# Split-weight products in a two-block layer kernel: three matmuls of 256 columns for each weight tile, in one half of a PSUM bank

## The reference

```
# first block
proj  = rms_norm(x) @ w_in;  mixed = g_nsa*(o_nsa @ w_up_nsa) + g_dn*(o_dn @ w_up_dn)
x     = x + mixed @ w_o
x     = x + (silu(h2 @ w_ffn_gate) * (h2 @ w_ffn_up)) @ w_ffn_down;   x = rms_norm(x)
# second block
proj  = rms_norm(x) @ w_in_2;  x = x + concat(y_rwkv, y_mla) @ w_out_2
x     = x + (silu(conv(h @ w_gate_2)) * (h @ w_up_2)) @ w_down_2;   return rms_norm(x)
```

## Time and profile before

| what | us |
|---|---|
| median of 3 runs | 2822.27 (2820.22 to 2822.9) |
| the profiled execution, its own time | 2820.33 |
| its span, first to last instruction | 2818.5 |
| TensorE busy with matmuls | 2771.2 (98%), 16660 matmuls |
| VectorE busy | 2023.7 (72%) |
| ScalarE busy | 1364.0 (48%) |
| GpSimd busy | 479.3 (17%) |

### The profile page before, as it was taken

One profiled execution on the slowest core, in us unless ns is written; L12 is line 12 of the kernel. 1 busy time (PEld: TensorE's weight loads), 2 busy tenths in 40 slices (PEclk: granted clock), 3 DMA queues, 4 the chain that ended last, 5 costly groups with the idle time before them and its releaser, 6 DMA issues.

```text
span 2818.5 us, 42260 instructions
## 1 busy us (share of the span) xinstructions
PE 2771.2 (98%) x16660; PEld 2434.1 (86%) x16660; DVE 2023.7 (72%) x3102; ACT 1364.0 (48%) x2051; POOL 479.3 (17%) x526
## 2 busy tenths in 40 slices
PE   8999999999999999999999999999999999999998
PEld 7888888888888888888888888878998888888887
DVE  7987797776776666656657888878677777667655
ACT  6453455455555445434435545434454444444434
POOL 2211011110111111001102635421111111001101
PEclk9999999999999999999999999999999999999999
DMA  6444333455555555555556534221365555555555
GB/s 227 162 160 159 121 116 132 145 191 188 193 187 190 192 191 191 192 190 193 188 183 199 177 124 133 92 76 53 120 202 191 191 192 189 193 188 194 189 180 164
DMA packets 133396, 474.65 MB, mean 168 GB/s; under 512 B 14800, under 2 KB 15056, under 8 KB 132944
## 3 DMA queue, kind: packets, MB, share of 16 engines
q1 hardware_dynamic: 133200, 471.96, 50.3%
HBM read 469.80 MB, written 2.10 MB: 167 GB/s over the span
## 4 chain that ended last, share of the span: by engine, by line
PE 90%; DVE 5%; ACT 2%; POOL 1%; issue 1%; DMA 0%; SPq 0%; DVEq 0%; ACTq 0%; POOLq 0%
PE ps L899 90%; DVE U L1869 1%; DVE ringl L1869 1%; POOL U L2551 1%; ACT high L1409 1%; PE ps L902 1%; POOL U L2624 0%; ACT U L1409 0%; DVE U L1878 0%; DVE xT L1869 0%; DMA xT<-in_x_dram 0%; DVE hx L1869 0%; DVE U L2067 0%; ACT hr L1409 0%; DVE U L1875 0%
## 5 line engine op out<-in xcount | busy, mean ns | idle before, releaser
L899 PE MATMUL ps<-hr,high 128*128 128x512 f32 x4672 | 1491.4, 397 | 11.8 <-DVE ringl L1869 10.8
L1869 DVE TENSOR_TENSOR ringl<-ring,high 128x1024 fp32r<-128x1024 f32 x888 | 1082.6, 1221 | 435.1 <-ACT high L1409 434.6
L1409 ACT ACTIVATE high<-ring 128x1024 fp32r<-128x1024 f32 x888 | 915.6, 1033 | 601.6 <-PE ps L899 590.7
L899 PEld LDWEIGHTS ps<-hr,ringl 128*128 128x128 f32 x4672 | 879.2, 188 | 192.5 <-issue 1.4
L899 PE MATMUL ps<-hr,ringl 128*128 128x256 f32 x4672 | 924.3, 279 | 0.0
L899 PEld LDWEIGHTS ps<-hr,high 128*128 128x128 f32 x4672 | 717.6, 188 | 21.0 <-issue 15.1
L899 PE MATMUL ps<-yur,high 128*128 128x512 f32 (+1 forms) x2432 | 682.9, 370 | 3.8 <-DVE xT L1869 2.2
L2551 POOL TENSOR_TENSOR U<-U,rs 128x256 f32<-128x256 f32 x292 | 264.5, 906 | 1688.3 <-DVE U L1869 1668.8
L899 PEld LDWEIGHTS ps<-yur,ringl 128*128 128x128 f32 x2176 | 400.0, 188 | 79.6
L1409 ACT ACTIVATE U<-ps 128x256 f32<-128x256 f32 (+3 forms) x481 | 172.8, 371 | 592.0 <-PE ps L899 567.6
L899 PE MATMUL ps<-yur,ringl 128*128 128x256 f32 x2176 | 429.9, 279 | 0.0
(11 more groups left out here) (178 smaller groups left out, 1250.2 us busy)
## 6 DMA issues: line engine op xcount, KB each, us to landing
ring<-in_w_dram SPq DMA_DIRECT2D x862, 512.0 KB, 3.3
ring<-in_w_dram SPq DMA_DIRECT2D x48, 256.0 KB, 3.3
xT<-in_x_dram SPq DMA_DIRECT2D x3, 512.0 KB, 8.1
out_dram<-hx SPq DMA_DIRECT2D x3, 512.0 KB, 2.7
cst<-in_cst_dram SPq DMA_DIRECT2D x1, 1374.5 KB, 12.5
yT<-in_lora_dram SPq DMA_DIRECT2D x1, 1024.0 KB, 7.4
xT<-in_x_dram SPq DMA_DIRECT2D x2, 256.0 KB, 4.5
U<-in_lora_dram SPq DMA_DIRECT2D x1, 512.0 KB, 5.4
```

What stands on the lines that cost most here:

```text
L899: return e.matmul(out, l, r, start=start, stop=stop)
L1409: return e.activation(out, i, ACT.Copy, scale=scale)
L1869: return e.tensor_tensor(out, a, b, op)
```

## The change

Every split product takes the narrow form. The high weights are used for two matmuls of 256 columns, over x's high half and over its low half; all three products of a tile are summed into half 0 of the bank. The order by pairs of tiles stays. Evacuation is then one step: ScalarE's copy signals `free` itself, VectorE's `rest` is gone, `wo` and `down` take one addition instead of two, and GpSimd's scaling waits for ScalarE instead of VectorE. For the units `up` VectorE waits for ScalarE's `free` before it multiplies with the gate. The planner's costs follow: TILE 0.348 to 0.342, ROWS 0.72 to 0.69 (the units with moving weights), and no additions of half 1 in VectorE's list. The number of weight tiles, the DMAs, the splits and the side chains stay as they are.

```diff
-TILE, TILE4, TILE33, ROWS = 0.348, 0.432, 0.23, 0.72
+TILE, TILE4, TILE33, ROWS = 0.342, 0.432, 0.23, 0.69
...
+            scaled_ = [u for u in ends if normed(u)]
+            added = [u for u in ends if sums_x(u)]
+            merged = [u for u in ends if u.kind == "up"]
...
-                                [("free" if one_half(u) else "half", u.i) for u in own] + [("data", u.i) for u in own if one_half(u)]))
-            work["DVE"].append((m - 0.5, sum(0.42 if u.kind == "wout" else 0.85 if sums_x(u) else 0.9 if u.kind == "up" else 0.43 for u in both_) + 0.4 * later.count("up"),
-                                [("end" if sums_x(u) else "half", u.i) for u in both_], [("free", u.i) for u in both_]))
-            work["POOL"].append((m - 0.5, 1.1 * len(both_), [("free", u.i) for u in both_], [("data", u.i) for u in both_]))
+                                [("free", u.i) for u in own] + [("data", u.i) for u in own if not normed(u)]))
+            work["DVE"].append((m - 0.5, 0.42 * len(added) + sum(0.9 if u.key[0] else 0.48 for u in merged) + 0.4 * later.count("up"),
+                                [("end", u.i) for u in added] + [("free", u.i) for u in merged], [("free", u.i) for u in added]))
+            work["POOL"].append((m - 0.5, 1.1 * len(scaled_), [("free", u.i) for u in scaled_], [("data", u.i) for u in scaled_]))
...
-                            c = mact if one_half(prev) else mdve
+                            c = mdve if sums_x(prev) else mact
                             e.wait_ge(c.sem, c.after("free", prev.i))
...
-                                if u.kind == "wout":
-                                    for n_, half in enumerate(moving(u, k0 + k)):
-                                        mm(out[:, 0:SEQ], wh, half, start and n_ == 0, False)
-                                else:
-                                    mm(shaped(out[:, :], 2, SEQ), wh, halves(u, k0 + k), start, False)
+                                for n_, half in enumerate(moving(u, k0 + k)):
+                                    mm(out[:, 0:SEQ], wh, half, start and n_ == 0, False)
...
-                copy(place_of(u), src).then_inc(mact.sem, mact.inc("free" if one_half(u) else "half", u.i))
+                copy(place_of(u), src).then_inc(mact.sem, mact.inc("free", u.i))
...
-            def rest(u, dst):
-
-                e.wait_ge(mact.sem, mact.after("half", u.i))
-                tt(dst, dst, ps[u.bank][:, SEQ:2 * SEQ], ADD).then_inc(mdve.sem, mdve.inc("free", u.i))
-
             def evac0(u):
                 key = u.key
-                if one_half(u):
-                    return
                 if u.kind == "up":
                     part, t = key
                     s = sg[t % 4]
-                    rest(u, um[:, t % 2, :])
                     e.wait_ge(mact.sem, mact.after("sig", 16 * part + t))
-                    e.wait_ge(mdve.sem, mdve.last())
+                    e.wait_ge(mact.sem, mact.after("free", u.i))
...
-                    parts = 1 if u.kind == "wout" else 2
-                    for j in range(parts):
-                        src = ps[u.bank][:, SEQ * j:SEQ * j + SEQ]
-                        if u.kind == "wo":
-                            i = stt(x, src, 0.5, x, MUL, ADD)
-                        else:
-                            i = tt(x, x, src, ADD)
-                        i.then_inc(mdve.sem, mdve.inc("free", u.i) if j == parts - 1 else mdve.inc())
-                        if j < parts - 1:
-                            e.wait_ge(mdve.sem, mdve.last())
+                    i = stt(x, src, 0.5, x, MUL, ADD) if u.kind == "wo" else tt(x, x, src, ADD)
+                    i.then_inc(mdve.sem, mdve.inc("free", u.i))
...
-                else:
-                    rest(u, place_of(u))
...
+                    e.wait_ge(mdve.sem, mdve.after("tb", f, t))
...
-                    e.wait_ge(mdve.sem, mdve.after("free", u.i))
+                    e.wait_ge(mact.sem, mact.after("free", u.i))
```

More of the change, by code:

```diff
@@ L766, in build, with normed @@
             needs[units[index[("rw", q, 0)]].first()] = [(f"rw{q % STREAMS}", (q // STREAMS - 2) * len(RECUR) + taken)]
-        def one_half(u):
-            return u.kind in ("cmpkc", "cmpvc", "vs", "vw", "uv", "uq", "uk")
         def sums_x(u):
             return u.kind in ("wo", "down", "wout")
+        def normed(u):
+            return u.kind in ("gates", "dn", "q", "kc", "vc", "ks", "kw", "mg", "gate", "fup", "lora", "rw", "lat")
         work = {"PE": [], "ACT": [], "DVE": [], "POOL": []}
@@ L800, in build @@
             own = [u for u in ends if not sums_x(u)]
-            both_ = [u for u in ends if not one_half(u)]
+            scaled_ = [u for u in ends if normed(u)]
+            added = [u for u in ends if sums_x(u)]
+            merged = [u for u in ends if u.kind == "up"]
             later = [u.kind for u in p.ends.get(m - 2, [])]
             work["ACT"].append((m - 0.5, 0.4 * len(own) + 0.4 * (later.count("mg") + later.count("up")), [("end", u.i) for u in own] + [("data", u.i) for u in p.ends.get(m - 2, []) if u.kind == "mg"],
-                                [("free" if one_half(u) else "half", u.i) for u in own] + [("data", u.i) for u in own if one_half(u)]))
-            work["DVE"].append((m - 0.5, sum(0.42 if u.kind == "wout" else 0.85 if sums_x(u) else 0.9 if u.kind == "up" else 0.43 for u in both_) + 0.4 * later.count("up"),
-                                [("end" if sums_x(u) else "half", u.i) for u in both_], [("free", u.i) for u in both_]))
-            work["POOL"].append((m - 0.5, 1.1 * len(both_), [("free", u.i) for u in both_], [("data", u.i) for u in both_]))
+                                [("free", u.i) for u in own] + [("data", u.i) for u in own if not normed(u)]))
+            work["DVE"].append((m - 0.5, 0.42 * len(added) + sum(0.9 if u.key[0] else 0.48 for u in merged) + 0.4 * later.count("up"),
+                                [("end", u.i) for u in added] + [("free", u.i) for u in merged], [("free", u.i) for u in added]))
+            work["POOL"].append((m - 0.5, 1.1 * len(scaled_), [("free", u.i) for u in scaled_], [("data", u.i) for u in scaled_]))
             work["POOL"].append((m, 0.0, [("used", m - 1)] if 0 < m <= M else [], []))
@@ L877, in place_of @@
             return (flat if u.kind == "uq" else kn)[:, key[0], :]
-        def normed(u):
-            return u.kind in ("gates", "dn", "q", "kc", "vc", "ks", "kw", "mg", "gate", "fup", "lora", "rw", "lat")
         rs_read = {"norm2": index[("mg", 1, 15)], "attn_g": index[("fup", 1, 43)], "ffn_g": index[("rw", 7, 2)],
                    "final_g": index[("fup", 2, 43)]}
[L887 to L891, removed]
         block = ctx.enter_context(nc.Block())
@@ L1922, in evac0 @@
                         mdve.also("sg", 16 + t)
-                elif u.kind in ("wo", "down", "wout"):
-                    x = xT[:, key[-1], :]
+                elif sums_x(u):
+                    x, src = xT[:, key[-1], :], ps[u.bank][:, 0:SEQ]
                     e.wait_ge(used.sem, used.after(u.end()))
```

## The result

The kernel before took 2821.24 us (median of 4 executions, 2819.47 to 2822.90), the changed one 2868.48 us (median of 4, 2866.27 to 2870.67): 1.0168 times as long, 95% interval 1.0150 to 1.0185. The forecast was 2790, in the range 2778 to 2818; the change costs 47 us instead of giving 32.

A forecast was written before the change was run, and what follows sets the result against it. The prediction took TensorE's matmul stream as the bound. Gains of 25.7 us in pure stream, 4.5 among side work and 2 from evacuation made 32 us less, a forecast of 2790 us, range 2778 to 2818.

The forecast's parts named there:

- What bounds the kernel: Whole span: TensorE, busy 98% at full clock, sets the time by its number of matmuls times their starting pace.
- The counts: Main stream: 6592 tiles, 3296 pairs, change form; 6592 more matmuls, 23252 in all, none of 512 columns in that stream.
- The pace of a pair: Main stream: a pair of tiles changes by between -11 and +15 ns from 0.690 us; 10.5 ns less taken for pure stream.
- the 2446 pairs in pure stream: Stretches of main stream alone, mostly feed-forward: each pair 10.5 ns shorter, 25.7 us less in all.
- The 850 pairs among side work: Mixed stages: each pair gains half the pure-stream amount, 5.3 ns, 4.5 us less in all.
- (c): Rival: w_out_2's first part, 117.5 ns a matmul, shows the narrow form's pace; +48 us, 2870 us; chance 0.04.
- (b): Rival: each matmul has a fixed cost besides its columns, so the third one slows a tile; 2839 us; chance 0.06.
- Evacuation: Emptying PSUM: VectorE loses 182 us of additions, hidden in pure stream; 2 us less in all, between 0 and 8.
- The planner's order: Mixed stages: side steps move against the main stream, a few microseconds to either side; taken as 0.

## Why the prediction was wrong, by its own steps

**What bounds the kernel**: right. TensorE's stream set the time before and after, no wait took its place, and the time moved with the pace of the starts. One reading was too smooth: a 9 in the clock's line of the earlier trace rows is 90% or more, and between 434 and 442 us the clock of the kernel before was at 0.57.

**The counts**: right, 23252 matmuls, none of 512 columns, 3296 pairs.

**The pace of a pair, the step that failed.** The prediction bounded it at -11 and +15 ns from two places of w_out_2 and took -10.5, because the second part "has the same blocks, no side work, and low inputs at the same kind of places". Measured over the feed-forward parts: 6 x 117.8 - 690 = +16 to +17 ns, just past the other bound. With 3296 pairs that is 53 us if every pair ran so; the account gives 39, and w_o and parts of 620 to 730 us did run at 113.33. That is the term of 25.7 us less for the 2446 pairs in pure stream, with its sign wrong. What was wrong was not an omitted cost: the narrow form's 113.33 was real, and is read in the same place after the change. It was one of two paces of the same instructions, and one stretch of 60 us, a single unbroken run of the stream, was taken as 530 samples where it was one. In three of the later kernels that very stretch, at the same distance, ran at 117.78, so it was chance that the trace of before showed it fast. The two places of the earlier trace rows disagreed by 4%, in a trace whose wide form repeats its mean pace within 0.3 ns a matmul from one feed-forward part to the other (900 / 5210 against 700 / 4058 us); that disagreement was the finding, and I explained it away by side chains and shared blocks. `vs`, which I counted as a second witness, reads its operands the other way round, so it was no witness for this distance.

**The 850 pairs among side work**, -5.3 ns each: wrong in sign too. Among the side work most restarts came out slow.

**The rivals.** (c), given 0.04, named the size: +48 us, 2870, against 2868. That it is so close is in part luck: it has all 48 from the pace, which gave 39, and knows nothing of the middle stretch's part. Its wording, that the slow pace is the narrow form's own and the fast one the exception, holds for distance 16 in 91 of 101 stretches, but not as a property of the form: at 48 the first feed-forward part runs at 113.33. (b), a fixed cost for each matmul, 2839, is not what was seen: one form has paces from 113.3 to 120.0 at one count of matmuls, by place alone. The Trainium skill, "TensorE: Matmul & The Clock Gate", section "Back-to-back issue gap", gives N / 2.4 + 2.5 ns as the gap of an isolated matmul, which comes to 109.2 for 256 columns. The runs show 113.3 to 120.0, and nothing in that formula depends on where the operands lie.

**Evacuation**, 2 us less: not found. VectorE fell by 125 us and not by 182; the additions went as counted (`xT` from 224 to 128), but its other steps grew longer, the remainders written into `yur` from 419 to 675 ns on the mean, with idle time before them for ScalarE's rounding. None of it matters in a stream that doesn't wait for VectorE, as the prediction said. GpSimd's scalings are released by ScalarE, as foreseen.

**The planner's order**, taken as nothing: it cost. With the new evacuation the side chains' part grew and the clock fell to half for some 20 us from 1968 us on; against the run with the split alone it is 8 us, 6 in the profiled executions. The prediction allowed "a few microseconds to either side" of idle time and left out that a TensorE that idles more can lose its clock as well.

**Left open.** Why splitting the matmul brings these paces at all, and what picks 113.33 or 117.78 at distances 16 and 48. The places of the moving operand decide which paces exist. In the feed-forward parts two executions of one program made the same choice and four ways of disturbing the stream changed nothing; among side work and in w_out_2 the choice changed with neither the instructions nor their places. At 113.33 throughout, the 20736 matmuls of the changed kernel would take 20736 x (117.45 - 113.33) = 85 us less, about 2783; no run came there. Distances at other values than those in the table, other alignments of `high` against `ringl`, and weights and inputs moved together, which would tell the distance from the place, weren't tried.

## What to carry to other kernels

When two places of one trace show the same instructions at paces that differ by more than the stream's own jitter, take them for two paces that both exist, and put the chance on each by how many separate stretches show it, not by how many matmuls: here one clean run of 530 outweighed everything and was the minority. Before replacing one wide matmul by two narrow ones in a stream that is bound by TensorE, run that single line; it cost 38 us here with the rest untouched. And treat the place of the moving operand in SBUF as a tuning value: the same program ran from 2838 to 2918 us by it alone.

## What the runs showed of the hardware that was not expected

- The distance from start to start of a 256-column float32r matmul, with a weight load for each and TensorE never idle at the full clock, depends on the place of the moving operand, here given by its distance from the weights: 120.0 ns at 0 and 24 columns, 116.7 at 8, 113.3 or 117.8 at 16 and 48, 118.7 at 32, 117.3 to 118.3 at 40, 118.3 at 56; 80 is as 16.
- At 16 and 48 the stream has two paces, 113.33 and 117.78 ns, and keeps one through as many as 6335 matmuls without a break: 746 us at the slow one from 820 us in the changed kernel, 718 us at the fast one from 817 us at distance 48. The same 623 matmuls of w_out_2 at the same distance ran at 113.33 in five kernels and at 117.78 in three.
- In the wide form, at distance 16, the next start comes 228 ns behind a 512-column matmul if it is another such and 231 ns behind if it is a low one, and 115 to 117 ns behind a low one. So one wide and one narrow take 345 ns a tile, and three narrow ones 340 or 353.
- TensorE's clock fell to the lower of its two levels (0.50 to 0.55 granted, 1970 to 1990 us) at the end of a stretch in which it had been busy 7.34 of 10 us, and was back at 1.00 from 1990. In the kernel before it stayed at 1.00 through 7.95 and 8.27 of 10 us.
